# Weight sums by halves, and three elementwise operations of a feed-forward unit on GpSimd

## The reference

```
def swiglu(x, w_gu, w_down):
    gate, up = jnp.split(x @ w_gu, 2, axis=-1)
    return (jax.nn.silu(gate) * up) @ w_down
x = x + 0.5 * swiglu(rmsnorm(x, norm), w_gu, w_down)   # D_MODEL 1024, D_FF 2816, eight times in all
```

## Time and profile before

| | |
|---|---|
| median of three runs | 2014.6 us (2014.39 to 2016.54) |
| the profiled execution: time, span | 2014.43 us, 2012.7 us |
| TensorE, VectorE, ScalarE, GpSimd busy | 99%, 84%, 62%, 9% |
| chain that ended last | TensorE 74%, VectorE 12%, ScalarE 7% |

### The profile page before, as it was taken

One profiled execution on the slowest core, in us unless ns is written; L12 is line 12 of the kernel. 1 busy time (PEld: TensorE's weight loads), 2 busy tenths in 40 slices (PEclk: granted clock), 3 DMA queues, 4 the chain that ended last, 5 costly groups with the idle time before them and its releaser, 6 DMA issues.

```text
span 2012.7 us, 25302 instructions
## 1 busy us (share of the span) xinstructions
PE 1987.9 (99%) x10204; PEld 1686.0 (84%) x10204; DVE 1681.1 (84%) x1570; ACT 1243.4 (62%) x1318; POOL 186.5 (9%) x180
## 2 busy tenths in 40 slices
PE   8999999999999999999999999999999999999998
PEld 6888998888888899988888888988888878998887
DVE  7997568997999689969987997779988997568996
ACT  6665576565666566646666665446665665576664
POOL 1001001010000014411001010001001000001010
PEclk9999999999999999999999999999999999999999
DMA  9896535896797484368986895758986896535992
GB/s 294 273 269 212 168 105 149 273 266 216 230 270 227 156 265 127 127 230 228 279 266 167 272 260 185 213 186 230 284 259 176 267 267 216 174 105 143 276 262 104
DMA packets 250632, 436.65 MB, mean 217 GB/s; under 512 B 10924, under 2 KB 93188, under 8 KB 250004
## 3 DMA queue, kind: packets, MB, share of 16 engines
q1 hardware_dynamic: 215876, 363.39, 53.1%
q0 software_dynamic: 34496, 71.39, 19.7%
q10 hardware_dynamic: 144, 0.26, 0.0%
HBM read 433.92 MB, written 1.08 MB: 216 GB/s over the span
## 4 chain that ended last, share of the span: by engine, by line
PE 74%; DVE 12%; ACT 7%; issue 4%; DMA 2%; SPq 0%; DVEq 0%; POOLq 0%; POOL 0%; ACTq 0%
PE bank L1630 38%; PE bank L1771 23%; PE bank L1636 8%; DVE w_lo L1134 6%; ACT w_hi L751 6%; PE bank L1805 2%; DVE stage L1274 2%; DVE arena L1497 2%; DVE arena L1274 1%; DMA stage<-in_ffn_w_gu 1%; PE bank L1663 1%; DMA arena<-in_ffn_w_gu 1%; PE bank L1976 1%; PE bank L1948 1%; PE bank L1958 0%
## 5 line engine op out<-in xcount | busy, mean ns | idle before, releaser
L1134 DVE TENSOR_TENSOR w_lo<-stage,w_hi 128x2048 fp32r<-128x2048 f32 (+1 forms) x245 | 562.3, 2299 | 89.3 <-ACT w_hi L751 86.9
L751 ACT ACTIVATE w_hi<-stage 128x2048 fp32r<-128x2048 f32 (+1 forms) x245 | 462.9, 1893 | 222.1 <-PE bank L1630 106.3
L1134 DVE TENSOR_TENSOR w_lo<-arena,w_hi 128x2048 fp32r<-128x2048 f32 (+1 forms) x199 | 450.5, 2268 | 80.2 <-ACT w_hi L751 78.5
L751 ACT ACTIVATE w_hi<-arena 128x2048 fp32r<-128x2048 f32 (+1 forms) x199 | 376.7, 1897 | 184.9 <-PE bank L1630 87.3
L1630 PE MATMUL bank<-w_hi,mt_hi 128*128 128x512 f32 x928 | 366.8, 395 | 0.4 <-DVE mt_lo L1383 0.4
L1630 PE MATMUL bank<-w_lo,mt_hi 128*128 128x512 f32 x928 | 361.7, 390 | 0.0
L1630 PE MATMUL bank<-w_hi,mt_lo 128*128 128x512 f32 x928 | 361.0, 390 | 0.0
L1771 PE MATMUL bank<-w_hi,mt_hi 128*128 128x512 f32 x512 | 205.3, 401 | 8.0 <-DVE w_lo L1134 7.9
L1636 PE MATMUL bank<-xt_hi,w_hi 128*128 128x256 f32 x704 | 204.1, 291 | 1.2 <-DVE arena L1497 0.7
L1630 PEld LDWEIGHTS bank<-w_hi,mt_lo 128*128 128x128 f32 x928 | 174.3, 188 | 36.7
L1630 PEld LDWEIGHTS bank<-w_hi,mt_hi 128*128 128x128 f32 x928 | 174.5, 188 | 35.2 <-DVE mt_lo L1383 0.8
(11 more groups left out here) (222 smaller groups left out, 2956.3 us busy)
## 6 DMA issues: line engine op xcount, KB each, us to landing
arena<-in_ffn_w_gu SPq DMA_DIRECT2D x82, 1024.0 KB, 5.7
stage<-in_ffn_w_gu SPq DMA_DIRECT2D x78, 1024.0 KB, 5.3
stage<-in_ffn_w_down SPq DMA_DIRECT2D x100, 512.0 KB, 5.2
arena<-in_ffn_w_down SPq DMA_DIRECT2D x76, 512.0 KB, 5.0
arena<-in_ffn_w_gu POOLq DMA_DIRECT2D x35, 1024.0 KB, 9.0
stage<-in_ffn_w_gu POOLq DMA_DIRECT2D x29, 1024.0 KB, 10.1
arena<-in_ffn_w_gu SPq DMA_DIRECT2D x20, 512.0 KB, 6.7
arena<-in_sb_w_qkv SPq DMA_DIRECT2D x16, 512.0 KB, 4.6
```

Source lines behind the costliest of these rows:

```text
L751: act.activation(w_hi[q][:, 0:c], stage[s][:, 0:c], ACT.Copy).then_inc(hi_done, 1)
L1134: dve.tensor_tensor(w_lo[q][:, 0:c], stage[s][:, 0:c], w_hi[q][:, 0:c].bitcast(F32), ALU.subtract).then_inc(lo_done, 1)
```

## The change

It does four things in the feed-forward phases.

1. At junctions the sum for A1 is made in two halves of 1024 columns, and ScalarE's copy to `w_hi` and VectorE's subtraction to `w_lo` follow in halves (semaphores `sum_half`, `hi_half`, `lo_half`). Both halves of the subtraction stand right behind the sums in VectorE's list. TensorE starts A1 on the first half and waits for the second before its seventh product.
2. The second gate (`sg[1] = p57 - p16`) of every S unit goes from VectorE to GpSimd (`second_gate`).
3. Both products of hid by sg of every S unit go to GpSimd (`gated_product`). At junctions the order on GpSimd is second gate, first product, A3's transfer, A2's transfer, second product. Behind the last S unit of a phase it is second gate, first product, second product.
4. ScalarE's second SiLU now follows the first directly, behind A2's release, and waits for GpSimd.

```diff
+def junctions_to(f, u):
+    return f * sum(adjacent(v) for v in range(len(UNITS))) + sum(adjacent(v) for v in range(u + 1))
+HALF = (slice(0, 1024), slice(1024, 2048))
...
@@ GpSimd
+            def second_gate(p, u):
+                f, sums = nth("ffn", p), sums_before(nth("ffn", p), u)
+                pool.wait_ge(gated, 2 * (N_UNITS * f + u))
+                pool.wait_ge(part_summed, 4 * sums + 1)
+                pool.wait_ge(part_copied, 3 * sums + 3)
+                pool.tensor_tensor(sg[:, 1, :], p57, p16, ALU.subtract).then_inc(gate_summed, 1)
+            def gated_product(p, u, h):
+                f, sums = nth("ffn", p), sums_before(nth("ffn", p), u)
+                pool.wait_ge(silu_done, 2 * (N_UNITS * f + u) + h + 1)
+                pool.wait_ge(part_summed, 4 * sums + (2, 4)[h])
+                pool.tensor_tensor(hid[:, h, :], hid[:, h, :], sg[:, h, :], ALU.mult).then_inc(gated, 1)
...
+                    if adjacent(u):
+                        second_gate(p, u - 1)
+                        gated_product(p, u - 1, 0)
                     pool.wait_ge(w_summed, 2 * sums_before(nth("ffn", p), u) + SUM_STEP["A1"])
                     pool.dma_start(stage[other][:, :].rearrange("p (k c) -> p k c", k=4), b22,
                                    accum_op=ALU.add).then_inc(a3_in, 16)
                     pool.wait_ge(lo_done, base[p] + FFN_ORDER.index((u, "A1")) + 1)
                     pool.dma_start(stage[to][:, :].rearrange("p (k c) -> p k c", k=4), b22,
                                    accum_op=ALU.add).then_inc(a2_in, 16)
+                    if adjacent(u):
+                        gated_product(p, u - 1, 1)
+                    if not adjacent(u + 1):
+                        second_gate(p, u)
+                        gated_product(p, u, 0)
+                        gated_product(p, u, 1)
...
@@ ScalarE
+                if name == "A1" and adjacent(u):
+                    act.wait_ge(block_used, n - SPLIT_SLOTS + 1)
+                    act.wait_ge(sum_half, junctions_to(nth("ffn", p), u))
+                    act.activation(w_hi[q][:, HALF[0]], stage[s][:, HALF[0]], ACT.Copy).then_inc(hi_half, 1)
+                    act.wait_ge(w_summed, len(SUM_STEP) * sums + SUM_STEP[name])
+                    act.activation(w_hi[q][:, HALF[1]], stage[s][:, HALF[1]], ACT.Copy).then_inc(hi_done, 1)
+                    return
...
                     if name == "A2":
                         silu_summed(u, 0)
-                        if not adjacent(u + 1):
-                            silu_summed(u, 1)
-                    elif name == "A4" and adjacent(u + 1):
                         silu_summed(u, 1)
...
@@ VectorE
-                def hidden_summed(u, h):
-                    dve.wait_ge(silu_done, 2 * (N_UNITS * f + u) + h + 1)
-                    dve.wait_ge(part_summed, 5 * sums_before(f, u) + (2, 5)[h])
-                    dve.tensor_tensor(hid[:, h, :], hid[:, h, :], sg[:, h, :], ALU.mult).then_inc(gated, 1)
...
+                    dve.tensor_tensor(w("B11")[:, HALF[0]], w("B12")[:, HALF[0]], w("B11")[:, HALF[0]],
+                                      ALU.add).then_inc(sum_half, 1)
+                    dve.tensor_tensor(w("B11")[:, HALF[1]], w("B12")[:, HALF[1]], w("B11")[:, HALF[1]],
+                                      ALU.add).then_inc(w_summed, 1)
...
+                    dve.wait_ge(hi_half, junctions_to(f, u))
+                    dve.tensor_tensor(w_lo[q][:, HALF[0]], stage[s][:, HALF[0]], w_hi[q][:, HALF[0]].bitcast(F32),
+                                      ALU.subtract).then_inc(lo_half, 1)
+                    dve.wait_ge(hi_done, n + 1)
+                    dve.tensor_tensor(w_lo[q][:, HALF[1]], stage[s][:, HALF[1]], w_hi[q][:, HALF[1]].bitcast(F32),
+                                      ALU.subtract).then_inc(lo_done, 1)
...
                         if name == "B11" and adjacent(u):
-                            weight_sum(u, "A1")
-                            second_gate(u - 1)
-                        elif i >= 1 and FFN_ORDER[i - 1][1] == "A4" and adjacent(FFN_ORDER[i - 1][0] + 1):
-                            hidden_summed(FFN_ORDER[i - 1][0], 1)
+                            weight_sum_by_halves(u)
+                            split_by_halves(u, b0 + i + 3)
...
@@ TensorE
+                    if name == "A1" and adjacent(u):
+                        pe.wait_ge(lo_half, junctions_to(f, u))
+                    elif n > 0:
                         block_in(n)
...
+                        if k == whole_from:
+                            block_in(n)
```

More of the change, by code:

```diff
@@ L1764, in plain_block, with product @@
                     mm.then_inc(block_used, 1)
-                def product(n, out_, x_, start, stop):
+                def product(n, out_, x_, start, stop, whole_from=None):
                     for k in range(4):
+                        if k == whole_from:
+                            block_in(n)
                         x, w = x_(k), w_pair(n, 512 * k, 512)
@@ L1832, in ffn @@
                         pe.wait_ge(xs_lo_done, 4 * (f + 1))
-                        product(n, bank[5], x_sum_part(0), True, True)
+                        product(n, bank[5], x_sum_part(0), True, True, 2 if adjacent(u) else None)
                     elif name == "B22":
```

30 lines of the change are left out of this document (17 added, 13 removed).

## The result

The changed kernel takes 2057.1 us (median of 4 runs, 2055.4 to 2058.9) against 2014.6 us before: a ratio of 1.0208, 95% interval 1.0194 to 1.0223. The forecast was 2062. Its profiled span is 2054.6 us, 41.9 longer than before.

The account below looks back on a forecast made before the run. TensorE, busy 99%, was taken as the bound, so late GpSimd products add time: 2014.4 + 34 (junctions) + 13.5 (unit ends) = 2062 us. Its own range was 2040 to 2080, chance 0.66; the overall range 2011 to 2084.

Parts of the forecast that it names:

- the unit ends: Behind each phase's last unit with sums, three GpSimd operations in a row delay the transposes +1.7 us, 8 times: 13.5 us.
- Steps 1 to 4: First junction: second gate, SiLUs, first product to 65.82, half sums held to 66.91 and 68.05; A1 on time at 70.19.
- The SSD pair: Earlier trace's GpSimd operations: 1.13 us once VectorE's two-input operation ends; VectorE's held subtraction ends 2.16 after GpSimd's end.
- Step 5: GpSimd's queue at a junction: the DMA issue takes 1.26 us, 70.69 to 71.95, with the second gated product behind it.
- step 6: VectorE starts B22's `w_lo` at 71.47; GpSimd, 0.5 us too late, waits for 73.76 and delivers the second product at 74.90.
- GpSimd slips into the gap: Rival, chance 0.12: second product issued before 71.4 ends by 72.5; junctions win 0.63 each: 1999, or 2013 with unit ends lost.
- TensorE has 3 us of slack: In the gap rival: B22's subtraction would be held instead of the transposes, and TensorE could absorb 3 us of that.
- Step 7: TensorE's transposes at a junction load at 74.95, against 73.54 before: +1.41 us, 24 times.
- the junction term: The loss of step 7 over all junctions: 24 x 1.41 = 34 us.
- is any of it given back?: Question on the junction's +1.41 us, answered with all later steps hanging on TensorE and the full 24 x 1.41 counted.
- a falling clock: Sign of being wrong: the clock, which never left its upper level, falls at the new 2 us gaps.
- the gain of the halves: At junctions, removing A1's stall on `w_lo` could win at most 0.63 us each, 24 x 0.63 = 15 us.

Follow-up runs that it names:

- writes-only run: The changed kernel with each GpSimd gate and product replaced by two memsets, its output not the reference's: 2014.6 us, ratio 0.9998.
- first product behind the transfer: The changed kernel with the first gated product of a junction moved behind A3's transfer in GpSimd's queue: 2055.2 us, ratio 1.0199.
- product ahead of the transfer: The changed kernel with the second gated product of a junction in front of A2's transfer on GpSimd: 2065.0 us, ratio 1.0247.
- last product on VectorE: The changed kernel with a junction's second product and all three operations behind a phase's last unit on VectorE: 2047.8 us, ratio 1.0167.
- A3's transfer later: The halves with all arithmetic on VectorE, plus A3's transfer at junctions waiting for the first half of A1's `w_lo`: 2074.3 us, ratio 1.0288.
- both products between the transfers: The changed kernel with both gated products of a junction behind A3's transfer and ahead of A2's on GpSimd: 2158.9 us, ratio 1.0717.
- the GpSimd part alone: The changed kernel with A1's sum, copy and subtraction whole as before, gate and products still on GpSimd: 2076.7 us, ratio 1.0305.

## Why the prediction was right, and where it was not

The kernel is slower by 2.1%, inside the range that the prediction gave its own case (2040 to 2080). The steps up to A1 and the unit ends came as named; the junction lost its time in another form than named, and that the number came near is in part luck. Step by step:

**Steps 1 to 4 held.** The trace runs 0.06 us behind the times named. First product until 65.90 (65.82 named), half sums until 66.98 and 68.11 (66.91, 68.05), last half of A1's `w_lo` until 70.53 (70.39), A1 on time. The SSD pair of the earlier trace rows carried over: 1.16 us behind VectorE's end for GpSimd (64.74 to 65.90), and 2.17 behind GpSimd's end for the held one. The writes-only run shows it by its absence.

**Step 5 failed in its size.** The issue's row is 1.29 us, but the next instruction's row starts 0.78 behind its start (70.83 to 71.61), not 1.26. So step 6 fell too: the product was not 0.5 us late for the gap but level with VectorE's subtraction (71.52), and it went first. This is the mechanism of the rival "GpSimd slips into the gap". It came true, and its price was wrong: "TensorE has 3 us of slack" for B22's subtraction, and in the main sum "B22, whose `w_lo` is long there". Unheld, that subtraction ends at 73.8, and B22 wants it some 1.1 us behind the transposes of 72.9, so about 74.1: a slack of 0.3. I had it from no row. Held, it ended at 75.59.

**Step 7** therefore has another form than named: not one wait of about 2.0 us a junction but 0.53 for the transposes and 1.30 for B22. The sum of both less the 0.75 of before is 1.08; the unit grew by 1.10 at the first junction. Named was 1.41, so the junction term was 34 us by the sum and is 24 x 1.08 = 26. The form as predicted can be seen in the run with the first product behind the transfer: transposes at 74.91 (named 74.95), and its unit is 32.82, also 1.11 longer. Here lies the luck: by these two runs who went first decided the form of the wait and hardly its price, so an error in the order at the port cost the sum nothing, while the rival that had the order right gave 2013. Part of such a wait is given back at once: B22's first load follows the transposes by 0.82 us where they waited and by 1.14 where they didn't (before, 73.54 to 74.68). So "is any of it given back?" should have been answered with 0.3 of 1.41.

**The unit ends** were named +1.7 each, 13.5 us; measured +1.72 to the transposes, and 14.4 us when they are undone. Junctions and unit ends make 26 + 14 = 40 of the span's 41.9. The other 2 are the one fall of the clock: the spacing that it lies in is 34.75 us, where its neighbours have 32.8. The prediction had named a falling clock as a sign of being wrong; once in 24 junctions it fell, behind waits of 1.09 and 1.30 us.

**What the prediction didn't see** is the loop. It looked at A3's transfer and gave it slack until A3, and named A2's only as something in the queue. With the gate and first product on GpSimd, A3's issue moves 1.48 us, and at the first junction the loop alone gives 32.8 us a unit, as much as the holds do; over the 16 spacings the loop's sum is 32.4 in the mean, 0.4 below the 32.8 that the holds give. So it sets little of the change's own time, but it stands right behind the holds, and it is nearer still when they go. That is why taking away one limit gained nothing. Where the holds behind A1 were cut (product ahead of the transfer; last product on VectorE), the loop took over: 8 us more, and 2047.8 against the 2042.7 of the kernel that has only the unit ends on VectorE. Where the loop was cut (first product behind the transfer), the holds stayed: 2 us less. It is also why the gain of the halves, 15 us by the first paragraph of the prediction, was 8.5: the loop closes at 31.48 in the first junction and in ten of the 16 spacings.

**What stays open.** What decides who gets the port when both come within 0.2 us: GpSimd won with its row 0.09 behind VectorE's (71.61 and 71.52) and lost with 0.22 and 0.59 behind (72.16 and 71.94; 72.05 and 71.46), but rows don't show when an instruction asks. What the middle leg is made of, one transfer behind the other or all the traffic of busy DMA engines, and why it differs by up to 2 us between the junctions of one kernel and by 1 us in the mean between kernels.

## What to carry to other kernels

Before work is moved to an idle engine, list what else is in that engine's queue and what starts from there: here one DMA issue 2.0 us later at each junction, with nothing else changed, cost 68 us, some of them through falls of the clock. Where a kernel is periodic, work out each closed loop through a period (issue, landing, the engine's row behind it, the next issue) and its length; a stall that is removed wins only down to the next longest loop. Read a loop over all its periods: the first junction shows it closed, and 14 of 16 spacings of the changed kernel don't. Give every consumer that is called "long there" a row and a number.

## What the runs showed of the hardware that was not expected

- A DMA issue's row of 1.29 us on GpSimd holds its queue for about 0.8 us only (70.83 to 71.61 in the change; 67.22 to 68.03 and 71.23 to 72.05 in the run with the first product behind the transfer).
- Two accumulating transfers of 1 MB on GpSimd's queue, with other traffic beside them, finish as if one behind the other: at the first junctions the second is there 15.7 to 16.4 us after the first's issue, whether it is issued 0.9 us later (A3's transfer later), 2.4 or 4.3 (before); issued 7.6 later, it took 20.9. Over all junctions of these runs but the last it was 14.7 to 17.8.
- Memsets on GpSimd neither wait for VectorE's two-input operations nor hold them (0.53 us for 128x512).
- Granted clock. In the run with both products between the transfers, busy time and granted clock in stretches around A2's first wait (columns as above):

```profile
89.00:93.00 4.00, 1.09 (x5) 0.56 (x3) 4.00 (x3) 3.59 (x3) 0.00 (x0) 1.00 0.11 41
93.00:97.00 4.00, 3.87 (x10) 3.12 (x11) 4.00 (x5) 1.62 (x1) 0.00 (x0) 0.57 0.71 238
97.00:101.00 4.00, 4.00 (x20) 3.27 (x19) 3.11 (x3) 3.27 (x4) 1.33 (x1) 1.00 0.84 287
```

After a stretch in which TensorE was busy 1.09 of 4 us the granted clock was 0.57 of full over the next four, most of them at its lower level, 1.2 GHz, and then in full again. In those four TensorE finished 10 matmuls where the next four have 20, so a wait of 3.46 us costs about two more behind it. Shorter waits seldom did it: with 24 waits of about 2.1 us the clock didn't fall between the ends of the trace (first product behind the transfer), with as many of 2.2 it fell once for 3.4 us (the GpSimd part alone), and in the change once, behind waits of 1.09 and 1.30 us close together.
